# A hybrid decoder layer on one core: the order of all weight transfers written out, gate transfers and two small MLPs placed inside other chunks

## What is computed

```
proj = einsum('btd,df->btf', x, w_in)              # 4096 -> h, bg, cg, z_conv, q, k_cmp, v_cmp, 4 x kv, z_att, 48 gate logits
y_conv = (bg * causal_conv3(cg * h)) * silu(z_conv)
kc, vc = compress_blocks(k_cmp, ...), compress_blocks(v_cmp, ...)
   # blocks of 32 tokens + pos -> (4096 -> 128) MLP: silu(block @ w1) @ w2
o_cmp, o_slc, o_win = attention on compressed, selected and window keys, 16 heads, 4 KV groups
y_att = sum_b sigmoid(gate_b) * o_b * silu(z_att)
out = concat(y_conv, y_att) @ w_out
return layer_norm(2 ** 0.25 * x + out, ln_g, ln_b)
```

## Time and profile before

| what | value |
|---|---|
| median of 3 runs | 1754.35 us (1753.48 to 1756.15) |
| the profiled execution's own time | 1756.29 us |
| its span, first to last instruction | 1754.7 us |
| PE busy | 1738.4 us, 99% |
| PE weight loads, DVE, ACT, POOL busy | 82%, 69%, 45%, 4% |
| mean granted TensorE clock | 0.995 |
| mean DMA rate | 195 GB/s |

### The profile page before, as it was taken

How to read it: one execution, slowest core, us unless ns; L and a number is a source line. 1 busy time by engine, 2 the same in 40 slices (tenths; PEclk the granted TensorE clock), 3 DMA queues, 4 the chain that set the end, 5 groups by cost and what they waited for, 6 DMA issues and landing times.

```text
span 1754.7 us, 24194 instructions
## 1 busy us (share of the span) xinstructions
PE 1738.4 (99%) x7895; PEld 1444.4 (82%) x7895; DVE 1211.4 (69%) x1859; ACT 793.0 (45%) x960; POOL 74.9 (4%) x101
## 2 busy tenths in 40 slices
PE   9999999999999999999999999999999999999997
PEld 7888888888888888888888888888888888888885
DVE  6666658887665688866568887656788865555555
ACT  5464444444444544444445444444545343333343
POOL 2000000000000000000000000000000021111112
PEclk9999999999999999999999999999999999999998
DMA  9676666656676666667665656766556776666664
GB/s 298 191 228 181 193 194 177 191 169 193 196 195 195 182 180 180 180 194 202 193 192 171 189 169 181 216 193 193 178 169 191 240 227 212 206 207 204 204 192 145
DMA packets 236994, 341.76 MB, mean 195 GB/s; under 512 B 12092, under 2 KB 94380, under 8 KB 236748
## 3 DMA queue, kind: packets, MB, share of 16 engines
q1 hardware_dynamic: 234720, 333.49, 64.2%
q0 software_dynamic: 2160, 6.79, 1.1%
HBM read 336.04 MB, written 4.19 MB: 194 GB/s over the span
## 4 chain that ended last, share of the span: by engine, by line
PE 97%; DVE 1%; DMA 1%; ACT 0%; SPq 0%; POOL 0%; issue 0%; POOLq 0%; DVEq 0%
PE bank L1113 31%; PE bank L1115 31%; PE bank L1114 31%; DMA raw<-in_w_in 1%; PE bank L1120 0%; PE bank L1310 0%; PE bank L1292 0%; PE bank L1290 0%; PE bank L1291 0%; DVE parts L742 0%; DVE a_t L732 0%; PE bank L1308 0%; PE bank L1306 0%; PE bank L1200 0%; PE bank L1307 0%; PE bank L1370 0%
## 5 line engine op out<-in xcount | busy, mean ns | idle before, releaser
L742 DVE TENSOR_TENSOR parts<-raw,parts 128x1024 fp32r<-128x1024 f32 x614 | 759.8, 1244 | 475.9 <-ACT parts L573 471.1
L573 ACT ACTIVATE parts<-raw 128x1024 fp32r<-128x1024 f32 x614 | 648.2, 1061 | 809.1 <-PE bank L1115 783.8
L1113 PE MATMUL bank<-parts,xt_hi 128*128 128x512 f32 x1912 | 747.0, 391 | 0.3 <-DVE xt_lo L732 0.3
L1115 PE MATMUL bank<-parts,xt_lo 128*128 128x512 f32 x1912 | 744.7, 390 | 0.0
L1114 PE MATMUL bank<-parts,xt_hi 128*128 128x512 f32 x1912 | 744.6, 389 | 0.0
L1115 PEld LDWEIGHTS bank<-parts,xt_lo 128*128 128x128 f32 x1912 | 359.1, 188 | 75.3
L1113 PEld LDWEIGHTS bank<-parts,xt_hi 128*128 128x128 f32 x1912 | 359.3, 188 | 74.5 <-DVE xt_lo L732 0.5
L1114 PEld LDWEIGHTS bank<-parts,xt_hi 128*128 128x128 f32 x1912 | 359.4, 188 | 73.4
L1113 PE MATMUL bank<-parts,mix_hi 128*128 128x512 f32 x512 | 199.6, 390 | 0.0
L1114 PE MATMUL bank<-parts,mix_hi 128*128 128x512 f32 x512 | 199.2, 389 | 0.0
L1115 PE MATMUL bank<-parts,mix_lo 128*128 128x512 f32 x512 | 199.2, 389 | 0.0
(11 more groups left out here) (167 smaller groups left out, 693.8 us busy)
## 6 DMA issues: line engine op xcount, KB each, us to landing
raw<-in_w_in SPq DMA_DIRECT2D x418, 512.0 KB, 3.7
raw<-in_w_out SPq DMA_DIRECT2D x128, 512.0 KB, 4.4
raw<-in_w_in SPq DMA_DIRECT2D x132, 256.0 KB, 3.2
x_tok<-in_x SPq DMA_DIRECT2D x16, 256.0 KB, 6.8
x_res<-in_x POOLq DMA_DIRECT2D x8, 512.0 KB, 4.5
out_y<-y SPq DMA_DIRECT2D x16, 256.0 KB, 2.3
raw<-in_cmp_w_k SPq DMA_DIRECT2D x4, 512.0 KB, 4.8
raw<-in_cmp_w_v SPq DMA_DIRECT2D x4, 512.0 KB, 4.7
```

Of the source, the lines that this page charges most:

```text
L573: act.activation(w_hi[s][:, :], raw[s][:, :], ACT.Copy).then_inc(s_hi, 1)
L742: dve.tensor_tensor(w_lo[s][:, 0:width], raw[s][:, 0:width], as_f32(w_hi[s][:, 0:width]), ALU.subtract).then_inc(s_lo, 1)
L1113: pe.matmul(acc, xh, wl, start=first and k == 0, stop=False)
L1115: mm = pe.matmul(acc, xl, wh, start=False, stop=last and k == GK - 1)
```

## The change

All loops are gone: one list, `ring_order()`, names every granule of the program in order, and each engine walks through it. There k is a granule of the keys' inputs, v of the values' inputs, g of the gates, m of an MLP, w of a group and o of the output.

- Gate granules g0 to g3 stand behind v2 to v5, the keys' MLP granules behind v10 to v13, the values' MLP granules behind granules 8 to 11 of the first group's ZA chunk.
- The gates' matmul has `xt_hi` and `xt_lo` side by side as one moving operand of 512 columns (two pieces of 256), 8 matmuls a granule in place of 16 with 256 columns. The sum of the two halves is a new DVE operation on `gate_t`.
- `a_transposes(0)` moves from v4 to v5, `a_high(0)` from v4 to v6, `a_low(0)` from v4 to v7, the conv taps' transpose from v8 to v9.
- The pass over zeros through gate and conv at the first group's start (DVE, ACT) is left out, with its three memsets.
- The banks of the chunks alternate the other way round.

```diff
+    order = [("k", 0, j) for j in range(GC)]
+    for j in range(GC):
+        order.append(("v", 0, j))
+        if 2 <= j < 6:
+            order.append(("g", 0, j - 2))
+        if 10 <= j < 14:
+            order.append(("m", 0, j - 10))
+    for g in range(NKV):
+        for i in range(CH * GC):
+            order.append(("w", g, i))
+            if g == 0 and 8 <= i < 12:
+                order.append(("m", 1, i - 8))
+    return order + [("o", c, j) for c in range(NOUT) for j in range(GC)]
...
-PAIR = (1, 0, 1, 0, 1, 0, 2)
+PAIR = (0, 1, 0, 1, 0, 1, 2)
...
@@ ACT: value_step(j) @@
+                if j == 6:
+                    a_high(0)
+                if j == 8:
+                    act.wait_ge(s_used, through("g", 0, 3))
+                    act.activation(gate_t[:, :], bank[0][:, 0:T], ACT.Copy).then_inc(gate_t_in, 1)
...
@@ DVE: value_step(j) @@
+                if j == 0:
+                    dve.wait_ge(s_small, small)
+                    a_tokens(0)
+                if j == 7:
+                    a_low(0)
+                if j == 9:
+                    dve.wait_ge(gate_t_in, 1)
+                    dve.tensor_tensor(gate_t[:, :], bank[0][:, T:2 * T], gate_t[:, :], ALU.add
+                                      ).then_inc(gate_t_in, 1)
...
@@ PE: gate granule, value_step(j) @@
-                for k in range(8):
-                    for m in (xt_lo, xt_hi):
-                        mm = pe.matmul(bank[0][:, 0:T], w_hi[n % RING][:, k * P:(k + 1) * P], m[:, 8 * j + k, :],
-                                       start=j == 0 and k == 0 and m is xt_lo,
-                                       stop=j == 3 and k == 7 and m is xt_hi)
+                for k in range(8):
+                    mm = pe.matmul(bank[0][:, :].rearrange("p (a t) -> p a t", a=2),
+                                   w_hi[n % RING][:, k * P:(k + 1) * P], xt[:, :, 8 * j + k, :],
+                                   start=j == 0 and k == 0, stop=j == 3 and k == 7)
...
+            def value_step(j):
+                if j == 5:
                     a_transposes(0)
-                if i == GC + 8:
+                if j == 9:
                     pe.wait_ge(s_small, small)
                     pe.wait_ge(a_l, 4)
                     transpose(bank[6][:, 0:48], conv_rows[:, :]).then_inc(taps_ps, 1)
+                if j == 10:
+                    pe.wait_ge(gate_t_in, 2)
+                    for t in range(TT):
+                        last = transpose(bank[0][:, t * P:(t + 1) * P], gate_t[:, t * P:(t + 1) * P])
+                    last.then_inc(gates_ps, 1)
```

More of the change, by code:

```diff
@@ L409, in _ @@
                 load_halves(n)
-            for n in range(HALVES, PRO):
+            for n in range(HALVES, len(ORDER)):
                 if n >= RING:
                     sp.wait_ge(s_lo, n - AHEAD)
-                first_loads(n)
+                load_granule(n)
                 if n + 1 < XP:
                     x_piece(n + 1)
[L417 to L444, removed]
             for i in range(FIN):
@@ L623, in evacuate, with mix_high @@
+            def mix_high(g):
+                for b in range(2):
+                    act.wait_ge(y_in.sem, y_in.at(g, b + 1))
+                    act.activation(mix_hi[:, KT // 2 + 4 * g + 2 * b:KT // 2 + 4 * g + 2 * b + 2, :],
+                                   conv[:, 2 * b:2 * b + 2, :], ACT.Copy).then_inc(y_hi.sem, 1)
             def evacuate(dst, func, c, g, done):
@@ L696, in affine_high @@
                                ).then_inc(affine_hi, 1)
[L698 to L704 removed]
+            for n, (kind, g, i) in enumerate(ORDER):
+                if kind == "k" and AHEAD <= i + HALVES < XP:
+                    x_high(i + HALVES)
+                if kind == "v":
+                    value_step(i)
+                if kind == "w":
+                    if g == 0:
+                        first_group_step(i)
+                    group_step(g, i)
+                if kind == "o":
+                    if g == 0 and i == 5:
+                        mix_high(NKV - 1)
+                    if i == 0 and g in (1, NOUT - 1):
+                        affine_high(g // (NOUT - 1))
+                if n + AHEAD < len(ORDER):
+                    split(n + AHEAD)
             def deviation(t):
@@ L1146, in a_transposes @@
                     last.then_inc(a_ps, 1)
-            def chunk_granules(base, g, per, hi, lo, pair, steps, j0=0):
-                for j in range(j0, GC):
-                    steps(j)
-                    n = base + j
-                    if base == GC and n >= MLP_K:
-                        n += 4
-                    pe.wait_ge(s_lo, g * per + (n + 1))
-                    granule(n, hi, lo, GK * j, pair, j == 0, j == GC - 1).then_inc(s_used, 1)
             def first_granule(n):
@@ L1255, in _ @@
-            last.then_inc(gates_ps, 1)
-            pe.wait_ge(hid_in, 2)
-            for g in range(NKV):
-                mm = pe.matmul(bank[7][0:NC, g * HD:(g + 1) * HD], hid[:, 1, g, 0:NC], w2_sb[:, 1, :],
-                               start=True, stop=True)
-            mm.then_inc(vc_ps, 1)
+                if i == 4:
+                    a_transposes(1)
+                if i == 14:
+                    sum_parts(1, bank[6][:, 2 * HD:2 * HD + 64])
+                if i == GC * KV:
+                    pe.wait_ge(a_in, 8)
@@ L1262, in group_steps @@
+                if i == 17:
+                    pe.wait_ge(hid_in, 2)
+                    for g in range(NKV):
+                        mm = pe.matmul(bank[7][0:NC, g * HD:(g + 1) * HD], hid[:, 1, g, 0:NC], w2_sb[:, 1, :],
+                                       start=True, stop=True)
+                    mm.then_inc(vc_ps, 1)
             def group_steps(g, i):
-                if i == 0:
-                    pe.wait_ge(cv.sem, cv.at(g, 0))
-                if i == GC * KV:
-                    pe.wait_ge(gates_in, 1)
+                if g and i == GC * ZA:
+                    pe.wait_ge(u_tok.sem, u_tok.at(g, 0))
@@ L1267, in group_steps @@
+                if g and i == GC * KV:
                     pe.wait_ge(zc_tok.sem, zc_tok.at(g, 0))
```

781 lines of the change are left out of this document (380 added, 401 removed).

## The result

The changed kernel takes 1750.68 us (median of 16 runs, 1750.39 to 1751.0), the kernel before beside it 1754.65 us (16 runs, 1753.48 to 1757.09). The ratio is 0.9977, 95% interval 0.9969 to 0.9984: faster by 4.0 us or 0.23%. Forecast were 5.7 us less, 1748.6. The time lies 2.1 us above the point, inside the range for 8 in 10, and only 0.1 us inside the narrower range of the forecast itself (to 1750.8).

What follows compares the result with a forecast made beforehand. PE, busy 99% of the span, was taken to bound the kernel. Waits and clock -7.3, gates -0.4, returns +0.5, breaks +0.4, new wait +1.1 gave -5.7 us: 1748.6, own range 1746.8 to 1750.8, 8 in 10 1745.9 to 1752.6.

Steps and rivals of the forecast that it cites:

- The waits taken away: Prologue: PE's waits for the values' tokens, low parts and sums go, saving 0.83, 0.76 and 2.54 us.
- The half clock: Behind the wait for the sums, 6.43 us of PE work at half clock would run at full pace, saving 3.2 us.
- the `hid` wait: Prologue's end: one PE wait of 2.4 us for the copy of the MLP's sums, 2.54 us lost start to start.
- 8 granules in hand: Eight granules lie between a load and its use, so no wait for memory was counted.
- Rival 3: Memory starves the v and m granule pairs: -3.7 to -0.5 us, middle 1752.2, chance 0.08.
- Gates: Gate granules: 32 matmuls of 0.227 us replace 64 of 0.12, 0.4 us gained, no price for two pieces.
- Breaks and returns: Granules broken at three places cost 0.4 us; seven returns from small to large matmuls cost 0.5 us.
- The new wait: At the taps' transpose ahead of v9, PE waits 1.1 us for `a_low(0)`, bounds 0 and 2.4.
- Rival 1: The new wait at the taps' transpose isn't there or is short: -6.8 us, 1747.5, chance 0.10.
- Rival 2: The new wait pulls the clock down, losing 3.2 us: -2.5 us in all, 1751.9, chance 0.08.
- No loops: Writing out the loops was costed at nothing on PE, since the loops' edges showed no gap.
- rivals 4 and 5: Straight code starves PE, 0.2 us per packet, 1761.9, chance 0.07; loops hid a price, 0.6 us per edge, 1746.2, chance 0.03.

Runs made afterwards that it cites:

- E1: The kernel before, run again unchanged to see how its executions spread: 1754.72 us.
- E2: The kernel before with nine unused matmuls filling PE's wait for `hid` at the prologue's end: 1753.7 us, ratio 0.9995.
- E3: The kernel before with all loops written out on all engines, order kept: 1755.43 us, ratio 1.0005.
- E11: The kernel before with the loops of all engines but SP written out: 1753.94 us, ratio 0.9992.
- E8: The kernel before with DVE's copy of the values' MLP sums one step sooner, ahead of a split: 1754.94 us, ratio 0.9999.
- E6: The changed kernel with the gates' matmuls at 256 moving columns again, 64 in number: 1751.04 us.
- E4: The changed kernel with the taps' transpose ahead of v11 in place of v9, and DVE's copy two steps later: 1750.59 us.
- E5: The changed kernel with the taps' and the gates' transposes both ahead of v11 and their follow-up work later: 1749.49 us, ratio 0.9971.
- E7: The changed kernel with `a_low(0)` one DVE step later, which lengthens PE's wait ahead of v9: 1752.13 us.
- E12: E5 with SP's walk through groups 1 to 3 and the output chunks in loops again: 1748.8 us, ratio 0.9968.
- E10: The kernel before with the loops of SP alone written out: 1756.65 us, ratio 1.0013.
- E9: E8 with ACT's copy of the gates and its SiLU also ahead of the split: 1752.8 us, ratio 0.9989.

## Why the prediction was right on the mechanism and off in size

*The waits taken away* went as forecast. None of the three is left, and the clock is full to the layer norm. Between the profiled executions the forecast of -5.7 met -5.67, and that was in part luck: +0.9 for breaks and returns, which the traces don't show, stood in for +0.8 at the end that was put at nothing.

*The half clock, 3.2 us.* This is the term that was mis-sized, together with the sentence that the profiled execution is "1.9 over the median; I take the difference over". For that execution the traces give 2.8 us, and for the median one filling the wait gave 1.0 us (E1, E2). The profiled execution of before was 1.64 us above the median of 16 (those of E1, E3 and E11 are the slowest or second slowest of theirs, too, so this may be more than chance), that of after lies on its median (1750.62 and 1750.68). So -5.67 in profiles is -5.67 + 1.64 + 0.06 = -3.97 in medians. A constant excess should have been doubted from the table of times alone: three runs of before spread over 2.7 us, and part of what the change removes (the dip of the clock) is what can differ between executions.

*What the `hid` wait was.* I took the wait's size from the trace, which was enough for the sum, but named its releaser, the copy, as its cause. The cause was a load that landed late, since it was issued late behind `a_low(1)` (E8). With it my view on memory was incomplete: I compared rates, where the time of issue decided, and that hangs on DVE. The "8 granules in hand" are in hand only while DVE keeps up. Rival 3 had it the wrong way round: the wait for a load was in the kernel before. In the pairs of after PE never waited for one.

*Gates*, -0.4: 0.36 in E6. The operand in two pieces of 256 costs nothing.

*Breaks and returns*, +0.9 in all: too dear. Of the -7.3 - 0.4 the lead on PE keeps 6.46 us, behind a new wait that takes 92.48 - 90.98 = 1.50 from start to start in place of 0.23, that is 1.27. So 7.7 - 1.27 - 6.46 leaves about 0, and about 0.15 if one counts that after began its k2 that much sooner (16.91 and 17.06). With 2.8 us for the dip in place of 3.2, the remainder falls by another 0.4, below zero; so the traces show no cost of breaks at all. The 0.07 for a return and the 0.13 for a break were estimates from one place each.

*The new wait*, +1.1: 1.10 us, at the place and time worked out. The next one that the prediction named, the sum on `gate_t` with 0.4 us to spare, was indeed next (it ended at 94.93, T+18.2, for T+18.4 forecast): taking the first away gave the second (E4), and only both together gave 1.2 us (E5). Rival 1 is out. Rival 2 is out at 1.1 us, but not by much: at 2.2 us the executions split (E7).

*No loops*, 0: wrong by 0.8 us, which the run of the loops alone shows with little certainty (E3, +0.8) and the ends of the profiles with more: 0.6 behind the last store from SP's straight program (3.36 in place of 2.79, and given back in E12), 0.2 outside of the span from the other engines' (E10, E11). PE itself has no gain or loss over 1330 us, so rivals 4 and 5 are both out. The pass over zeros was put at nothing since PE didn't wait beside it. That held for the order of before alone: in E9, with PE sooner, it cost 1.3 us. So leaving it out was probably needed for the gain; no run of the changed kernel with the pass in it shows how much. The Trainium skill ("Runtime: NRT & Kernel Launch", "Instruction fetch mechanics") has a taken branch to code outside of the prefetched window stall the engine, and full unrolling as what kernels prefer where possible. This case's runs don't agree with it as far as the time goes: +0.8 with all loops written out, +2.0 with SP's alone, -0.7 with all but SP's (0 is in the intervals of the first and the last), and 0.7 less when SP's are loops again in E5's order.

The bill by medians: waits -4.1, clock -1.0, gates -0.4, new wait +1.3, breaks +0.1, straight code +0.8, in sum -3.3, where -4.0 was measured. The 0.7 us that are left lie within the intervals of the terms (that of the clock alone is +-1.6); I can't place them for certain. An estimate from E1's table puts them in the clock's term: the nine executions of before at 0.997, a mean that only profiles with a full clock show, have a median of 1753.12, 2.4 above after, and the bill without the clock is -2.3; the clock would then be worth 1.5. E2, 0.6 above those nine, speaks against it.

The forecast's own range isn't what its bounds add up to. Added, they give 1746.6 to 1751.3, and not 1746.8 to 1750.8.

## What to carry to other kernels

Where PE is 99% busy, put whole granules of independent work between a small dependent piece and its producer, and after each wait removed look at once for the one that is late next: here only the second move paid. Follow a wait back past the instruction that released it until something was not waiting itself; a copy can be late because a load was, and the load because the engine that frees its slot was busy with something else. Work that costs nothing beside a late engine can cost something once that engine is sooner. And where the clock dips in a profile, look at many executions before you price the dip or carry the profile's excess over to the median.

## What the runs showed of the hardware beyond that

- The dip at the prologue's end differs between executions of the same program: 6.8 us at 1.2 GHz in one profile of before and 3.4 in the other. Behind one wait of 2.3 to 2.4 us it was 6.8 (before, E3, E11), behind one of 2.2 us 3.4 (E8) or nothing (E7). It doesn't take one long wait: 3.4 us followed 2.1 and 0.8 (E1), and also 1.5 and 1.3 (E10), in each case with a few small matmuls in between. A single wait of 1.0 to 1.2 us (after, E4, E9), and gaps of 0.6 to 0.7 us some 6 us apart, were followed by none in any profile.
- The time from the last store's issue to the span's end is 2.7 to 2.8 us in the seven profiles where SP's program has loops (before, E1, E2, E8, E9, E11, E12) and 3.3 to 3.4 us in the seven where it is straight (after, E3 to E7, E10). The stores are the same, and the last one takes that much longer to land; why the length of SP's program matters there stays open.
- Straight code on the other engines adds 0.2 us outside of the span (1.6 us without it, 1.8 with it: E10, E11 and E12).
